# A three-block model kernel on one core: first loads reordered over two queues, memory norm spread over chunks, one row of down weights kept for each last chunk, final gain applied ahead of the root

## The reference, cut to what matters

```python
def rms_norm(x, g):  return x * rsqrt(mean(x * x, -1) + 1e-6) * g
def swiglu(h, w_in, w_out):
    g, u = split(h @ w_in)            # 2816 columns each
    return (silu(g) * u) @ w_out
for layer in range(2):
    x = x + 0.5 * swiglu(rms_norm(x, g[0]), ffn1_in, ffn1_out)
    x = x + mixer(rms_norm(x, g[1]))  # even layer: two attentions; odd layer: convolution and banded attention
    x = x + memory_cross_attention(rms_norm(x, g[2]), rms_norm(mem, g[3]), ...)
    x = x + 0.5 * swiglu(rms_norm(x, g[4]), ffn2_in, ffn2_out)
# second block: x + mixers(rms_norm(x)); x + relu(rms_norm(x) @ w_ff1)**2 @ w_ff2; out = rms_norm(x) * norm_final
```

## Time and profile before

| | us |
|---|---|
| median of 3 runs | 1775.19 |
| lowest, highest | 1771.87, 1775.59 |
| the profiled execution's own time | 1773.97 |
| its span in the trace | 1772.4 |
| mean granted clock of TensorE | 0.983 of full speed |

### The profile page before, as it was taken

How to read it: one execution, slowest core, us unless ns; L and a number is a source line. 1 busy time by engine, 2 the same in 40 slices (tenths; PEclk the granted TensorE clock), 3 DMA queues, 4 the chain that set the end, 5 groups by cost and what they waited for, 6 DMA issues and landing times.

```text
span 1772.4 us, 21291 instructions
## 1 busy us (share of the span) xinstructions
PE 1679.6 (95%) x8135; PEld 1390.4 (78%) x8135; DVE 1116.7 (63%) x1742; ACT 851.1 (48%) x1287; POOL 256.6 (14%) x352
## 2 busy tenths in 40 slices
PE   5989998889999999999999999999998999999997
PEld 4878776678787887888789787888888778778886
DVE  4766688757466556555686574655566877765555
ACT  4544455355455445444545454544443345544443
POOL 2299703200000000000000000000044333100000
PEclk9999999899999999999999999999998999999999
DMA  8556755335255554555554443555564433545552
GB/s 229 178 179 208 227 144 170 119 104 170 96 174 179 182 190 155 190 190 187 186 174 144 149 159 107 178 185 190 186 218 122 123 107 119 178 166 187 183 187 97
DMA packets 184517, 293.10 MB, mean 165 GB/s; under 512 B 13422, under 2 KB 106000, under 8 KB 183520
## 3 DMA queue, kind: packets, MB, share of 16 engines
q1 hardware_dynamic: 180016, 275.40, 48.3%
q0 software_dynamic: 4400, 16.35, 3.1%
HBM read 286.19 MB, written 5.25 MB: 164 GB/s over the span
## 4 chain that ended last, share of the span: by engine, by line
PE 82%; DVE 9%; ACT 5%; issue 2%; POOL 1%; DMA 1%; SPq 0%; ACTq 0%; DVEq 0%; POOLq 0%
PE b L414 25%; PE b L416 24%; PE b L415 24%; DVE wlo L1475 3%; ACT whi L1000 2%; PE b L567 1%; ACT O L1021 1%; PE b L543 1%; PE b L530 1%; PE b L773 1%; PE b L789 1%; PE b L911 1%; PE b L479 1%; PE b L515 1%; ACT R L1069 1%
## 5 line engine op out<-in xcount | busy, mean ns | idle before, releaser
L1475 DVE TENSOR_TENSOR wlo<-raw,whi 128x1024 fp32r<-128x1024 f32 x522 | 649.1, 1245 | 516.6 <-ACT whi L1000 515.5
L1000 ACT ACTIVATE whi<-raw 128x1024 fp32r<-128x1024 f32 x522 | 549.8, 1055 | 638.1 <-PE b L416 635.4
L414 PE MATMUL b<-whi,hT 128*128 128x512 f32 (+1 forms) x1184 | 474.6, 401 | 18.6 <-DVE wlo L1475 12.1
L416 PE MATMUL b<-whi,hT 128*128 128x512 f32 (+1 forms) x1184 | 463.9, 392 | 0.0
L415 PE MATMUL b<-wlo,hT 128*128 128x512 f32 (+1 forms) x1184 | 463.2, 391 | 0.0
L414 PEld LDWEIGHTS b<-whi,hT 128*128 128x128 f32 x1184 | 226.5, 191 | 74.7 <-DVE wlo L1475 15.5
L414 PE MATMUL b<-whi,oT 128*128 128x512 f32 x672 | 264.7, 394 | 10.7 <-DVE oT L1556 10.4
L416 PEld LDWEIGHTS b<-whi,hT 128*128 128x128 f32 x1184 | 226.2, 191 | 47.6
L416 PE MATMUL b<-whi,oT 128*128 128x512 f32 x672 | 261.8, 390 | 0.0
L415 PE MATMUL b<-wlo,oT 128*128 128x512 f32 x672 | 261.6, 389 | 0.0
L415 PEld LDWEIGHTS b<-wlo,hT 128*128 128x128 f32 x1184 | 227.0, 192 | 43.0 <-issue 0.5
(11 more groups left out here) (291 smaller groups left out, 1784.7 us busy)
## 6 DMA issues: line engine op xcount, KB each, us to landing
raw<-in_ffn_w_in SPq DMA_DIRECT2D x352, 256.0 KB, 3.0
raw<-in_ffn_w_out SPq DMA_DIRECT2D x88, 512.0 KB, 3.3
raw<-in_w_ff SPq DMA_DIRECT2D x64, 512.0 KB, 3.3
raw<-in_w_in SPq DMA_DIRECT2D x40, 512.0 KB, 3.6
raw<-in_x_w_kv SPq DMA_DIRECT2D x32, 512.0 KB, 3.5
raw<-in_even_w_in SPq DMA_DIRECT2D x24, 512.0 KB, 4.1
raw<-in_odd_w_in SPq DMA_DIRECT2D x24, 512.0 KB, 3.8
raw<-in_x_w_q SPq DMA_DIRECT2D x16, 512.0 KB, 3.9
```

The costliest lines, as they stand in the source:

```text
L414: T.matmul(out, ah, bh, start=start, stop=False, skip_group_check=skip)
L416: return T.matmul(out, al, bh, start=False, stop=stop, skip_group_check=skip)
L1000: E.activation(K.whi[j % NSPLIT][:, 0:n], K.raw[j % NRAW][:, 0:n], ACT.Copy).then_inc(*S.whi.done(j))
L1475: V.tensor_tensor(K.wlo[j % NSPLIT][:, 0:n], K.raw[j % NRAW][:, 0:n], K.whi[j % NSPLIT][:, 0:n].bitcast(F32), ALU.subtract).then_inc(*S.wl ...
```

## The change

Start. SP issues `x` by column halves, the 128 columns of constants that hold the identity, weight piece 0, the second half of `x`, piece 1, the other constants (own semaphore `masks`, awaited by DVE in `trig_turns`), and then the pieces. ACT issues the ten loads into `rows`. POOL clears two columns and waits for piece 1 before its small loads and `mem`. ACT runs a tiny copy on the cleared columns. ACT and DVE split piece 0 ahead of the first norm; PE turns group 0 of `x` ahead of `rows`.

Memory norm. The squares stay at chunk 4 of f0 and chunk 2 of f1. `row_rstd` with `first_row` (DVE) goes to the chunk after, `second_row` (ACT) to the one after that, and the turns with their halves to the next two. Before, the first three stood at one chunk.

Last chunks of f0 to f3. Row 0 of `down(last-2)` stands behind `up(last-1)`, its row 1 behind `up(last)`, and `turn(last)` comes before the halves. The number of pieces is the same.

Order on ACT. At chunk 0 of every stage, and at `following`, `turned_halves` goes ahead of the squares.

End. DVE multiplies each quarter of the new `x` by the final gain right behind its addition. After the root, ACT scales the first 128 rows and DVE the others, in halves of 512 columns, and SP sends four quarters.

```diff
+def downs(f, c):
+    last = f.nch - 1
+    if f.gated and c >= last - 1:
+        return [(last - 2, [c - last + 1])]
+    return [(c - 1, list(range(f.per)))] if 0 < c < last else []
...
@@ pe_program, ffn
-            if 0 < c < last:
-                down(c - 1)
+            for chunk, rows in downs(f, c):
+                down(chunk, rows)
...
+        if f.gated:
+            turn(last)
...
-                    if (n, c, g) == (0, last - 1, 0):
+                    if (n, c, g) == (0, last - 1, 0) and not f.gated:
                         turn(last)
@@ pe_program, end
-    preamble()
-    norm_turns("f0", None, True, (0, 1))
-    ffn(FFNS[0], {1: trig_turn, 3: input_turn, 5: mem_turns(0, (0, 1)), 6: mem_turns(0, (2, 3))})
+    pe.wait_ge(*S.cst.at(0))
+    norm_turns("f0", None, True, (0,))
+    row_turn()
+    norm_turns("f0", None, True, (1,))
+    ffn(FFNS[0], {1: trig_turn, 3: input_turn, 7: mem_turns(0, (0, 1)), 8: mem_turns(0, (2, 3))})
-    ffn(FFNS[1], {3: mem_turns(1, (0, 1)), 4: mem_turns(1, (2, 3))}, "f2")
+    ffn(FFNS[1], {5: mem_turns(1, (0, 1)), 6: mem_turns(1, (2, 3))}, "f2")
@@ act_program, ffn
                 if p == 1 and c == 0:
+                    turned_halves(f.name, f.g0, K.hT, (2, 3))
                     x_squares(f.name, f.before, (1,))
-                    turned_halves(f.name, f.g0, K.hT, (2, 3))
...
-        weights(first + AHEAD)
+        if not f.gated:
+            weights(first + AHEAD)
         high(last)
         weights(first + 3 * groups - 1 + AHEAD)
         if following:
+            turned_halves(following, gain, K.hT, (0, 1))
             x_squares(following, f.name, (0,))
-            turned_halves(following, gain, K.hT, (0, 1))
         weights(first + 4 * groups - 1 + AHEAD)
@@ act_program, end
+    row_loads()
+    act.wait_ge(*S.zeroed.at("warm"))
+    E.activation(K.stat("warm", 2)[:, 1:2], K.stat("warm", 2)[:, 0:1], ACT.Copy).then_inc(*S.act_own.done())
+    weights(0)
-    ffn(FFNS[0], ..., {4: lambda: mem_rows(0), 5: mem_halves(0, (0, 1)), 6: mem_halves(0, (2, 3))})
+    ffn(FFNS[0], ..., {
+        4: lambda: mem_squares(0), 6: lambda: second_row("m0", K.M), 7: mem_halves(0, (0, 1)), 8: mem_halves(0, (2, 3))})
...
-    x_squares("end", "f4", (0, 1))
+    squares("end", K.x, lambda t, n: x_ready("f4", t, n), (0, 1), K.fs)
+    act.wait_ge(*S.rstd.at(("end", 0)))
+    for n in range(2):
+        act.wait_ge(*S.final.at((0, n)))
+        E.activation(K.O[:, 0, 512 * n:512 * n + 512], K.O[:, 0, 512 * n:512 * n + 512], ACT.Copy,
+                     scale=K.stat(("y", "end"), 2)[:, 0:1]).then_inc(*S.normed_a.done(("end", n)))
@@ dve_program
+    def end_gained(t, n):
+        V.tensor_tensor(K.O[:, t, cs], K.x[:, t, cs], K.M[:, 0, cs], ALU.mult).then_inc(*S.final.done((t, n)))
     def end():
         row_rstd("end")
-        for t in range(2):
-            V.scalar_tensor_tensor(out=K.O[:, t, :], in0=K.x[:, t, :], scalar=K.stat(("y", "end"), 2)[:, t:t + 1], in1=K.M[:, 0, :],
+        for n in range(2):
+            V.tensor_scalar(K.O[:, 1, cs], K.O[:, 1, cs], K.stat(("y", "end"), 2)[:, 1:2], None,
+                            ALU.mult).then_inc(*S.normed_d.done(("end", n)))
     preamble()
+    weights(0)
-        {1: trig_rows, 3: input_copies, 4: lambda: mem_rows(0), 5: mem_lows(0, (0, 1)), 6: mem_lows(0, (2, 3))})
+        {1: trig_rows, 3: input_copies, 5: lambda: mem_rows(0), 7: mem_lows(0, (0, 1)), 8: mem_lows(0, (2, 3))})
-    ffn(FFNS[1], {}, {2: lambda: mem_rows(1), 3: mem_lows(1, (0, 1)), 4: mem_lows(1, (2, 3))}, "f2", 40)
+    ffn(FFNS[1], {}, {3: lambda: mem_rows(1), 5: mem_lows(1, (0, 1)), 6: mem_lows(1, (2, 3))}, "f2", 40)
-    ffn(FFNS[4])
+    ffn(FFNS[4], after=end_gained)
@@ pool_program
+    E.memset(K.stat("warm", 2), 0.0).then_inc(*S.zeroed.done("warm"))
+    pool.wait_ge(*S.loaded[1].at(1))
     small_loads()
     mem_load(0)
@@ sp_program
-    for t in range(2):
-        Q.dma_start(K.x[:, t, :], D["x"]...[t]).then_inc(*S.x_in[t].done(0, step=16))
-    Q.dma_start(K.cst[:, :], D["consts"]).then_inc(*S.cst.done(0, step=16))
+    x_half(0)
+    Q.dma_start(K.cst[:, 0:P], D["consts"][:, 0:P]).then_inc(*S.cst.done(0, step=16))
...
+        if j == 0:
+            x_half(1)
+        elif j == 1:
+            Q.dma_start(K.cst[:, P:CONST_N], D["consts"][:, P:CONST_N]).then_inc(*S.masks.done(0, step=16))
```

More of the change, by code:

```diff
@@ L570, in turn, with down @@
                 free[b] = (S.alo.at((f.name, c, g)),)
-        def down(c):
-            for kk in range(f.per):
+        def down(c, rows):
+            for kk in rows:
                 hi, lo, j = piece(f.w_out, f.l, f.per * c + kk, 1, [(0, 1024)])
-                if kk == 0:
-                    K.first[f.name, "down", c] = j
+                K.first[f.name, "row", c, kk] = j
                 pe.wait_ge(*S.alo.at((f.name, c, kk // 2)))
@@ L984, in act_program @@
 def act_program(K, G, A):
[L986 removed]
+    S, E, D = K.S, K.nc.scalar, K.D
     act = Engine(E)
@@ L1012, in x_ready, with squares @@
     def x_ready(stage, t, n):
-        return S.x_in[t].at(0) if stage is None else S.added.at((stage, t, n))
-    def squares(name, src, ready, halves=(0, 1)):
+        return S.x_in[t][n].at(0) if stage is None else S.added.at((stage, t, n))
+    def squares(name, src, ready, halves=(0, 1), junk=None):
         ss = K.stat(("ss", name), 4).rearrange("p (t n) -> p t n", t=2)
@@ L1094, in down @@
         def down(c):
-            weights(K.first[f.name, "down", c] + f.per - 1 + AHEAD)
+            for chunk, rows in downs(f, c):
+                weights(K.first[f.name, "row", chunk, rows[-1]] + AHEAD)
         last, groups = f.nch - 1, f.per // 2
@@ L1117, in ffn @@
                 ins.then_inc(*S.silu.done((f.name, c, t)))
-            if 0 < c < last:
-                down(c - 1)
+            down(c)
             if c in extra:
@@ L1689, in project_x, with ffn @@
             added(stage, t, 1, K.place[f"{strips}1"][t], 1.0, S.dense.at((f"{strips}1", t)))
-    def ffn(f, beside={}, extra={}, following=None, gain=0):
+    def ffn(f, beside={}, extra={}, following=None, gain=0, after=None):
         def low(c):
@@ L1730, in ffn @@
                 added(f.name, t, n, 2 * t + n, f.scale, S.dense.at((f.name, t, n)))
+                if after:
+                    after(t, n)
     def mem_rows(l):
@@ L1758, in trig_turns @@
         dve.wait_ge(*S.trig.at("raw"))
+        dve.wait_ge(*S.masks.at(0))
         for t in range(2):
```

76 lines of the change are left out of this document (41 added, 35 removed).

## The result

The kernel after takes 1745.05 us (median of 5 runs, 1741.16 to 1750.66) against 1774.49 for the kernel before (median of 5, 1771.86 to 1775.59). The ratio over all runs is 0.984 (95%: 0.982 to 0.987), so it is faster by 27.9 us (24 to 32); the two medians are 29.4 apart. The forecast was 1750.4 with a range of 1744.5 to 1756.5. In a second series the same kernel took 1750.19. The five times follow the mean granted clock of their run: 0.982 in the slowest, 0.987 in the fastest.

A forecast was written before the change was run, and what follows sets the result against it. TensorE (PE), busy 95% of the span, was the bound; only its idle and low-clock time could be won. Terms 9.3 + 7.4 + 1.3 + 6.0 + 2.6 + 0.6 - 2.4 = 24.8 gave 1749.2 profiled, 1750.4 median (1744.5 to 1756.5).

The forecast's parts named there:

- the start: Kernel start: gains issued by ACT land at 7.6, first product at 10.6 instead of 19.88; 9.3 us saved (6.1 to 10.8).
- `following`: Where a stage follows at once: gain halves before squares on ACT lengthen PE's wait; 2.4 us lost (0 to 2.7).
- the signs that the prediction set: Included first product at 10 to 11, no 1.50 wait ahead of the last `down_half`, a 2.8 wait where 1.59 was.
- I cost all of it at nothing: At the start: POOL's small loads and `mem`, held until piece 1 is in, arrive before their first users; 0 us.
- The step that gave ACT's queue the credit: At the start: gains land 3.4 after their last issue, since nothing stands ahead in ACT's queue; landed at 7.6.
- Memory norm, f0: Chunks 4 to 6 of f0: spreading the norm removes PE's dry 5.14 and 2.5 of low clock; 7.4 saved (4 to 7.6).
- Rival (b): Memory norm of f0: DVE's root beside POOL still leaves PE dry; 3.2 us back, time 1753.6, chance 0.10.
- f1: Memory norm of f1: the chain of 2.8 fits under its cover, so the dry 1.34 goes; 1.3 us saved.
- Kept row: Last chunks of the four gated stages: PE's 1.50 wait for the last product's low half goes; 6.0 us saved.
- Halves before squares at chunk 0: Chunk 0 of all five stages: PE's 0.52 wait for the low half of group 2 goes; 2.6 us saved.
- The end: Kernel end: first output quarter ready at about 1767.7, so its transfer starts earlier; 0.6 us saved (0 to 1.3).

The follow-up runs named there:

- POOL at once: Kernel after, but POOL issues its small loads and `mem` at once, not waiting for piece 1; 1764.49 us.
- SP's old order: Kernel after, but SP loads all of `x` and all constants ahead of the weights; ACT still issues the gains, POOL still waits; 1740.8 us.
- gains on SP: Kernel after, but SP issues the ten gain loads, behind half of `x` and the identity, ahead of the weights; first product at 12.67, whole time not given.
- root at chunk 4: Kernel after, but in f0's memory norm DVE's root and first row stand at chunk 4, ACT's row at chunk 5; PE dry for 3.69, whole time not given.
- squares first: Kernel after, but at `following` ACT squares before the gain halves, as before the change; 1744.33 us (median of 4), ratio 0.983.

## Why the prediction was right, and where it was wrong

The time lay in the range, near its middle in one series (1750.19) and at its lower edge in the other (1745.05). The profiled execution, which the sum was made for, has 1750.66 against the forecast's 1749.2. That agreement is partly luck: the start had another cause than the working gave, `following` cost nearly three times its term, and several waits were worth more than their idle time, which made up for part of it. By the signs that the prediction set, the first product is on the edge (11.02, where 10 to 11 was right, and up to 12.2 in other runs); the others hold.

**Idle and busy.** The sum took 22.3 out of PE's idle time (24.8 less the 2.5 of clock behind the memory norm) and those 2.5 out of its busy time. Measured: 23.5 of idle, and a busy time that rose by 0.3. Up to the mark the terms give 9.3 + 7.4 + 1.5 + 0.5 = 18.7, and the kernel is 222.86 - 204.11 = 18.75 ahead. From there to the end they give 1.3 + 4.5 + 2.1 + 0.6 - 2.4 = 6.1, and it won 4.45 more.

**The start: the size right, the cause wrong.** 8.9 against 9.3 by the first product, whose time is 11.0 to 12.2 in the nine runs that leave this start as it is. The landing was put at 7.6 and came at 8.2, and at up to 9.4 in the nine. But the step "I cost all of it at nothing" on POOL's deferral failed: it is the largest single part that the runs found. With POOL at once, the gains land at 11.4, a later piece leaves PE dry for another 3, and 7.6 are lost at the mark, against 2.8 for SP's order and 2.5 for the gains on SP. (Each was taken out alone, so they need not add up.) The working looked for a late user of the deferred loads, and not for what those loads hold up while they run. No run takes the tiny copy on ACT, the early split of piece 0 or the early turn of `x` out alone. The step that gave ACT's queue the credit failed with it: behind half of `x` and the identity the gains land earlier on SP.

The rule of the Trainium skill that the prediction weighed ("DMA: Bandwidth & Descriptors", Issuing engines are not separate DMA queues) said that a second issuing engine saves issue time alone. In SP's old order the same ten loads landed at 8.9 from ACT, beside 1.5 MB in SP's queue, and at 5.41 + 6.61 = 12.0 behind it in one queue; only 1.3 of these 3.1 are in the issue (the last at 4.10 instead of 5.41). POOL's loads were deferred in the one and not in the other, so they share in the rest, and with POOL at once the landing was 11.4. From the last issue to the landing it is 4.0 to 5.3 in the nine runs and 4.8 in SP's old order, between the 3.4 that the prediction took and the 6.61 that it read out of the rule. What the rule leaves out is that the weights flow meanwhile. Whether the same page's turns between queues (Queues, rings and completion order) let the small loads overtake, these runs hardly show: the gains come in little ahead of their turn in the order of issue, and the identity lands at 4.86 to 5.53 with ACT's loads beside it and at 4.68 in the one run without.

**Memory norm, f0: size right.** 7.6 against 7.4. Which of the two causes counts was left open in the working; the runs put 3.69 of the 5.14 on DVE's chain beside POOL's long steps. Rival (b), that this chain would still leave PE dry, fell because POOL's steps at chunk 5 are short, as the prediction had it: the root took 3.7, between the 2.8 of an undisturbed one and some 6.6 in the earlier trace rows. **f1:** the 1.34 is gone; no run undoes it alone.

**Kept row: right** to the hundredth in its waits (four of 1.50), with no new wait at the last `up`. Each was worth 1.7 and not 1.5, for the reason given with that run. What came in its place at the end of f0 is 0.7 more of waiting for DVE's additions, because the shorter norm brings PE there while POOL's tables still run. No step had that.

**Halves before squares at chunk 0: right** in its waits, 2.15 in four stages, which were worth 3.1; the fifth, f0, has another start.

**`following`: the wait right, its price too small.** Forecast was a wait of about 2.8 where it was 1.59; it is 2.77 behind f1 and 2.76 behind f3, a loss of 2.4. The step that failed is "PE's wait grows by the squares less the overlap, about 1.2, behind f1 and behind f3: 2.4 lost (0 to 2.7)": it has no term for the clock. Behind the longer wait PE runs 6.29 us at 0.51, and 6.29 x 0.49 = 3.1 of that are lost. In four of the ten profiles with this wait they aren't. Behind f3 it is this:

```profile
1278.77:1285.00 6.23, 6.23 (x41) 6.23 (x42) 3.38 (x7) 2.62 (x8) 0.00 (x0) 0.75 0.61 187
```

6.23 x 0.25 = 1.6. The term was therefore about 2.4 + 4.7 = 7 instead of 2.4 in this profile (6.6 by the starts of the same matmuls), and 5.9 by the run with the swap undone. The prediction had the very pair of rows for it (the earlier trace rows: a dry 5.14 and then clock 0.50) and used it only where it took a wait away, not where it lengthened one.

**What the sum lacks.** With 4.7 of clock that no term had, the second part should have won 6.1 - 4.7 = 1.4, and won 4.4. The starts of the same matmuls, before less after, show where the rest is:

| behind the mark | forecast | by the starts |
|---|---|---|
| chunk 0 of f1 to f4 | 2.1 | 3.1 |
| memory norm of f1 | 1.3 | 1.6 |
| last chunks of f1 to f3 | 4.5 | 5.2 |
| into f2 and into the second block, waits and clock | -2.4 | -6.6 |
| other stretches at the lower clock | 0 | -1.6 + 1.7 |
| small differences | 0 | 0.5 |
| the end | 0.6 | 0.5 |
| sum | 6.1 | 4.4 |

So waits that went were worth 2.0 more than their idle time in the rows. The two other stretches are a new one at 981 (lost 1.6) and one at 1425 that is shorter than before (won 1.7). The one at 981 is in six of the thirteen profiles of the changed kernel and its variants. Why such a stretch comes in one run and not in the next stays open, and runs of one kernel differ by up to 10 us by them.

**The end: right**, 0.5 against 0.6; the first transfer was issued 0.7 behind the root's last step.

## What to carry to other kernels

Loads issued by POOL at the start can cost the first loads of the others more than their bytes let you think: hold them back until what PE starts on has landed. Ask of every deferred or moved transfer what it slows while it runs, and not only who waits for it. When two engines hand work to each other in a fixed order, look at both before you swap one: the halves-first order on ACT lost time until DVE took the matching lows first. Where an edit lengthens a wait of PE from some 1.6 to 2.8 us, price the slow stretch that can follow; where it came, it cost as much again as the wait, or more. And price a wait by the starts of the matmuls on both sides of it: here each cost about 0.24 more than the idle time in its row.

## What the runs showed of the hardware

- With POOL's loads at once, 0.72 MB of POOL's took 29.0% of the DMA engines' time in the first 16 us, when 2.71 MB of SP's took 58.3%. By these rows a megabyte of POOL's cost 1.9 times as much engine time. It isn't always so: in the kernel after, 0.19 MB of POOL's took 3.5% in the same time and 4.41 MB of SP's 82.7%, which is about the same for a megabyte.
- Ten small loads behind each other in one lightly loaded queue were in 1.2 us behind the last issue (5.23 to 6.48, gains on SP); it was 4.0 when weights flowed beside them (4.12 to 8.16, kernel after).
- ACT issues a small load in 0.28 to 0.57 us, about SP's pace (0.25 to 0.43).
- A DVE step on 2 columns beside a POOL step of 1.04 to 1.30 took 0.97 to 1.17 in three cases and ended within 0.03 of it (root at chunk 4); beside POOL steps of 0.23 to 0.26 it took 0.17 to 0.23.
- Successive 128x512 matmuls last 0.39 and start 0.23 apart at full clock. A wait of 0.52 between two of them cost 0.76, and one of 1.50 cost 1.74.
- Behind the wait of 2.76 to 2.79 into f2 the granted clock was 0.50 to 0.51 over 6.2 us in five profiles, 0.72 in one and 1.00 in four; behind 1.59 at the same place it was 1.00 in the kernel before and in squares first.
- The mean clock of whole runs of one kernel went from 0.982 to 0.987, and with it the time by 9.5 us. What makes a given stretch fall in one run and not in another wasn't found.
